# Convolution layers of a two-block network: one adding transfer per weight chunk, fewer tap sums begun on TensorE

## Chip, cores and metric

One core of a Trainium2 chip runs the whole program in one launch. The metric is the device time of one execution in microseconds (us); lower is better.

## What is computed

Two blocks on a sequence of 512 tokens with 1024 features, all in float32. The first block has four layers: a convolution layer (a), a forgetting attention (b), a short convolution (c), and a second convolution layer (a). The second block is a sparse attention with an MLP. The change touches only the two layers a:

```python
def conformer_conv_mixer(h, w_in, conv_w, conv_b, ln_g, ln_b, w_out):
    proj = h @ w_in                              # (512, 1024) @ (1024, 3 * 2048)
    val, glu_gate, z = jnp.split(proj, 3, axis=-1)
    u = val * jax.nn.sigmoid(glu_gate)
    u = causal_depthwise_conv(u, conv_w) + conv_b    # 31 taps per channel
    u = jax.nn.silu(layer_norm(u, ln_g, ln_b))
    return (u * jax.nn.silu(z)) @ w_out
```

## The kernel before

**Products in three parts.** Activations and weights are each split into a high part, rounded to the matmul's faster number format, and a low part, the rest. A product is three matmuls: high by high, high weight by low activation, low weight by high activation. The weights arrive in chunks of 1 MB (`specs`), which alternate between two raw slots in `WR`, two in `WH` and two in `WL`. A chunk of the layers a has two halves of 128 columns: in the first 16 chunks the gate's columns and the value's, in the next 8 two tiles of z.

`load_chunk` runs on the sync queue (SP) and fills a raw slot, as soon as the low parts of the chunk that lay there before are done. `split_hi` on ScalarE copies a half to `WH` (that is the rounding) and, for the halves named by `summed`, writes its negative to `WL` too. `split_lo` on GpSimd then makes the low part: for those halves by a transfer that adds the raw weights to `WL` (`dma_add`, 512 KB, semaphores `w_sum`), for the others by a subtraction (semaphore `w_lo`). `wait_low` is the wait of the readers, TensorE and the sync queue, for either. In before, both halves of the chunks 1 to 15 of a layer are done by transfers, of the z chunks the first half by a transfer and the second by a subtraction.

**The slots of a layer.** Channels lie on partitions, in 16 tiles of 128. The work runs in slots 0 to 32. In slot s below 16 TensorE makes the gate and the value of tile s (`gemm_low_last`: 16 matmuls with the high weights, then a wait, then 8 with the low), ScalarE the sigmoid, VectorE the product `U[s]`. In slots 16 to 29 TensorE makes z, one tile a slot; ScalarE writes its silu (`silu_z`). TensorE may start slot s once `U[s - 2]` is made.

**The convolution.** A tile's 31 taps are summed in one of two ways. Tiles in `CHAIN` are summed in a PSUM bank by VectorE, one `stt` a tap. The sum is begun either by ScalarE with one tap (`begins_scalar`) or, for the tiles in `PE_BEGINS`, by TensorE with two taps, as matmuls of `U` with diagonal matrices that ScalarE makes (`diagonals_scalar`). The tiles in `POOL_TAPS` are summed by GpSimd: ScalarE writes the product of each tap (`products_scalar`) into a ring of 7 buffers, and GpSimd adds it (`conv_gpsimd`). A tile there with fewer than 30 taps is shared: GpSimd adds so many, VectorE the rest. Finished tiles are turned on TensorE (`turn_u`) for the layer norm's moments on VectorE.

**What sets the order.** `conv_plan` writes down, before anything runs, which taps, adds, beginnings and turns fall in which slot: `room` taps for VectorE and `room` adds for GpSimd, alternating between at most two tiles. Every engine then runs its part of each slot in program order. On ScalarE a slot below 16 is: second half of the next chunk (high, negative), start of a tile, first half of the products, sigmoid, first half of the chunk after next, beginnings, second half of the products. In a z slot it is: a half chunk, `silu_z`, then all products. On GpSimd a slot below 16 is: transfer of the next chunk's second half, half of the adds, transfer of the first half of the chunk after next, the other adds. The functions in question are `summed` (L321), `wait_low` (L325), `split_hi` (L360), `split_lo` (L373), the constants (L888 to L892), `conv_plan` (L896) and `layer_a_gpsimd` (L1313).

Of the kernel before, what the change touches and what calls it, by code (L numbers as in the profile page):

```python
# [18 lines left out]
KE = E // P  # L19
# [3 lines left out]
PAD = TAPS - 1  # L23
# [97 lines left out]
def build_program(nc, x, a_norm, a_w_in, a_conv_w, a_conv_b, a_ln_g, a_ln_b, a_w_out, b_norm,  # L121
# [4 lines left out]
    with ctx:  # L126
# [15 lines left out]
        WL = sb("WL", 2 * 2048, F32R)  # L142
# [66 lines left out]
        specs = []  # L209
# [22 lines left out]
        FIRST_A = [0, 0]  # L232
# [61 lines left out]
        def raw_slot(i):  # L294
            return WR[:, slot_of(i) * 2048:(slot_of(i) + 1) * 2048]
# [21 lines left out]
        w_hi, w_lo = sig("w_hi"), sig("w_lo")  # L317

        w_sum = [[sig(f"w_sum{i}{n}") for n in range(2)] for i in range(2)]

        def summed(i, n):  # L321

            return i == 0 and n == 1 or any(f < i < f + KE + (KE // 2 if n == 0 else 0) or i == f + KE + KE // 2 + 1 for f in FIRST_A)

        def wait_low(eng, i, n):  # L325
            if summed(i, n):
                eng.wait_ge(w_sum[i % 2][n], i)
            else:
                eng.wait_ge(w_lo, i, n)
# [41 lines left out]
                        act.act(halves(WL, i)[n], r, ACT.Copy, scale=-1.0).then_inc(w_hi, i, n, "low")  # L371

        def split_lo(pool, i, which=(0, 1)):  # L373
            if i < len(specs):
                for n, (r, h, l) in enumerate(zip(halves(WR, i), halves(WH, i), halves(WL, i))):
                    if n not in which:
                        continue
                    if summed(i, n):
                        pool.wait_ge(w_hi, i, n, "low")
                        if two_runs(i):  # L380
                            l, r = (t.rearrange("p k c -> p (k c)") for t in (l, r))
                        pool.dma_add(l, r).then_inc(w_sum[i % 2][n], i, by=16)
                    else:
                        pool.wait_ge(w_hi, i, n)
                        pool.tt(l, r, h, ALU.subtract).then_inc(w_lo, i, n)
# [499 lines left out]

        POOL_TAPS = {2: PAD, 4: PAD, 7: PAD, 10: PAD, 12: 24}  # L888
        CHAIN = [i for i in range(KE) if POOL_TAPS.get(i, 0) < PAD]
        PE_BEGINS = CHAIN[3:]  # L890
        LAST_TAP = {i: PAD - 2 if i in PE_BEGINS else PAD - 1 for i in CHAIN}
        BY_PE = [(i, k) for i in PE_BEGINS for k in (PAD, PAD - 1)]  # L892
        POOLED = sorted(POOL_TAPS)
        Z_LATE = 3

        def conv_plan():  # L896
# [5 lines left out]
            for slot in range(2 * KE + 1):  # L902
                rest = slot == 2 * KE
# [18 lines left out]
                while begun < len(CHAIN) and begin() is not None:  # L922
                    at["begin"].append(CHAIN[begun])
                    open_.append(CHAIN[begun])
                    begun += 1
                room = PAD * KE if rest else (15) if slot < KE else (7)
                for n in range(room):
                    two = [i for i in open_ if taps[i]][:2]
                    if two:
                        i = two[n % len(two)]  # L930
# [3 lines left out]
                for i in POOLED:  # L934
                    if i < slot and i not in pooled and len([m for m in pooled if adds[m]]) < 2:
                        pooled.append(i)
                        at["start"].append(i)
                room = PAD * KE if rest else (8) if slot < KE else (3 + slot % 2)
                for n in range(room):
                    two = [i for i in pooled if adds[i] and (adds[i][0] < PAD or emptied.get(i, slot) < slot)]  # L940
                    if two:
                        i = two[n % len(two)]
# [370 lines left out]
        def layer_a_gpsimd(pool, j):  # L1313
            c0 = FIRST_A[j]
            normalise_gpsimd(pool, j)

            def pads():
                if j == 0:
                    biases_gpsimd(pool)
                    pool.wait_ge(bias_mm)  # L1320
                    pool.wait_ge(x0, KD - 1)
                else:
                    pool.wait_ge(p_out, 2, 7)
                    pool.wait_ge(x_new, 2, KD - 1)
                pool.memset(AR[:, 0:KE * UW].rearrange("p (i u) -> p i u", i=KE)[:, :, 0:PAD], 0.0).then_inc(
                    consts, "a_pads", j)

            if j:
                pads()
            for slot in range(2 * KE + 1):  # L1330
                n = PLAN[slot]["add"]
                if slot < KE:
                    split_lo(pool, c0 + slot + 1, (0, 1) if slot == 0 else (1,))
                    if j == 0 and slot == 0:
                        pads()
                    conv_gpsimd(pool, j, n[:len(n) // 2])
                    split_lo(pool, c0 + slot + 2, (0,))
                    conv_gpsimd(pool, j, n[len(n) // 2:])
                else:
                    m = (slot - KE) // 2  # L1340
                    if slot < 2 * KE - Z_LATE and slot % 2 == 0:
                        split_lo(pool, c0 + KE + m + 1, (1,))
                    elif slot < 2 * KE - Z_LATE and m + 2 < KE // 2:
                        split_lo(pool, c0 + KE + m + 2, (0,))
                    conv_gpsimd(pool, j, n)
            split_lo(pool, c0 + KE + KE // 2)
            for i in range(0, KE, 2):
                part_low(pool, 3 * j, i, U[i][:, PAD:])
                if i == 0:
                    split_lo(pool, c0 + KE + KE // 2 + 1)  # L1350
                if i >= 4:
                    split_lo(pool, c0 + KE + KE // 2 + i // 2)
            split_lo(pool, c0 + KE + KE)
            for k in range(KD):
                scale_gpsimd(pool, 3 * j + 1, SQUARES[3 * j + 1], k)
# [1633 lines left out]
```

## Time and profile before

| | us |
|---|---|
| time, median of 3 runs (2595.8 to 2599.55) | 2596.78 |
| the profiled execution | 2595.92 |
| its span, first to last instruction | 2594.2 |
| TensorE busy | 2549.5 (98%) |
| VectorE busy | 1509.1 (58%) |
| GpSimd busy | 1514.1 (58%) |
| ScalarE busy | 1231.4 (47%) |
| the 16 DMA engines, share of the span: queue of the sync engine | 31.0% |
| the same, queue of GpSimd | 10.0% |

PE is TensorE (PEld its loading of weights), DVE VectorE, ACT ScalarE, POOL GpSimd, SP the sync engine; a q behind it is that engine's queue. L64 is the line of the helper that issues every matmul, L70 that of every ScalarE operation, L73 that of every operation on two tensors, L81 that of VectorE's taps, L115 the adding transfer, L118 the weight load. `out<-in` names tiles: WR, WH and WL are raw, high and low weights, HH and HL high and low activations, AR the arena with `U`, the products and the sums, SQ and DG further product buffers, ps a PSUM bank. A group of equal instructions has a count (x8) and its whole stretch as its time. The granted clock of TensorE was 0.997 of the full 2.4 GHz on the mean. Layer 0 lies from about 40 to 320 us, layer 1 from about 1445 to 1733 us.

### The profile page before, as it was taken

To read this page: it belongs to the slowest core of one execution; us is meant where nothing else is said; L and a number is where in the kernel's file an instruction comes from. 1 tells how busy PE (TensorE), PEld (TensorE's weight loads), DVE (VectorE), ACT (ScalarE), POOL (GpSimd) and SP (SyncE) were. 2 spreads that over 40 slices of the span, in tenths; PEclk is the share of its full clock that TensorE was granted. 3 is DMA by queue.
4 is the path that set the end of the run, shared out by engine and by line. 5 is a ranking of instruction groups with operands and counts; after the bars stand their busy time and mean duration, and the time that the engine had idled before them with its cause. 6 is when DMAs were issued, how large, how long until landed. Compare 5 with 4: busy or idle time off the path is not lost.

```text
span 2594.2 us, 31715 instructions
## 1 busy us (share of the span) xinstructions
PE 2549.5 (98%) x12043; PEld 2053.2 (79%) x12043; DVE 1509.1 (58%) x2434; ACT 1231.4 (47%) x1944; POOL 1514.1 (58%) x935
## 2 busy tenths in 40 slices
PE   8999999999999999999999999999999999999998
PEld 6777787878777787888888877878876778788887
DVE  6999764165585714444450899976498743532202
ACT  5887644254564633222232688754335553422322
POOL 2999765444444366444455499966535547644653
PEclk9999999999999999999999999999999999999999
DMA  8776434434334123333333677543422242233221
GB/s 196 177 177 144 121 96 93 98 81 76 77 75 74 57 98 86 96 96 97 97 98 98 155 169 179 132 114 109 114 94 85 67 139 97 85 98 98 98 98 65
DMA packets 296439, 279.12 MB, mean 108 GB/s; under 512 B 17813, under 2 KB 258671, under 8 KB 296288
## 3 DMA queue, kind: packets, MB, share of 16 engines
q1 hardware_dynamic: 281472, 223.94, 31.0%
q0 software_dynamic: 14816, 53.16, 10.0%
q8 instruction: 96, 1.57, 0.3%
q14 instruction: 55, 0.45, 0.1%
HBM read 228.75 MB, written 5.84 MB: 90 GB/s over the span
## 4 chain that ended last, share of the span: by engine, by line
PE 82%; DVE 11%; ACT 3%; issue 2%; DMA 1%; POOL 1%; SPq 0%; DVEq 0%; POOLq 0%; ACTq 0%
PE ps L64 80%; DVE AR L81 4%; DVE AR L73 2%; DVE ps L81 2%; PE ps L67 2%; DVE HL L81 1%; ACT L70 1%; ACT AR L70 1%; ACT HT L70 1%; DMA WR<-in_a_w_in 1%; DVE X L73 1%; POOL AR L73 0%; ACT HH L70 0%; DVE ST L97 0%; SPq L118 0%
## 5 line engine op out<-in xcount | busy, mean ns | idle before, releaser
L73 POOL TENSOR_TENSOR WL<-WR,WH 128x1024 fp32r<-128x1024 f32 x324 | 818.7, 2547 | 763.1 <-ACT WH L70 763.1
L64 PE MATMUL ps<-HH,WH 128*128 128x512 f32 x3080 | 1224.9, 398 | 4.2 <-ACT HH L70 1.2
L64 PE MATMUL ps<-HL,WH 128*128 128x512 f32 x3080 | 1193.1, 390 | 1.3 <-DVE HL L81 1.3
L64 PE MATMUL ps<-HH,WL 128*128 128x512 f32 x3080 | 1094.4, 390 | 2.4 <-DMA WL<-WR 2.3
L64 PEld LDWEIGHTS ps<-HH,WH 128*128 128x128 f32 x3080 | 578.7, 188 | 146.8 <-issue 16.2
L64 PEld LDWEIGHTS ps<-HL,WH 128*128 128x128 f32 x3080 | 579.2, 188 | 126.6 <-issue 7.9
L64 PEld LDWEIGHTS ps<-HH,WL 128*128 128x128 f32 x3080 | 578.0, 188 | 124.4 <-DMA WL<-WR 2.8
L70 ACT ACTIVATE WH<-WR 128x1024 fp32r<-128x1024 f32 (+1 forms) x405 | 409.2, 1047 | 486.3 <-PE ps L64 443.0
L81 DVE SCALAR_TENSOR_TENSOR ps<-AR,CW,ps 128x512 f32<-128x512 f32 x654 | 454.5, 751 | 18.4 <-ACT ps L70 11.4
L73 POOL TENSOR_TENSOR AR<-AR 128x512 f32<-128x512 f32 x200 | 306.2, 1831 | 17.3 <-ACT AR L70 10.1
L70 ACT ACTIVATE AR<-ps 128x512 f32<-128x512 f32 (+3 forms) x265 | 132.0, 522 | 272.1 <-PE ps L64 175.9
L73 DVE TENSOR_TENSOR AR<-AR 128x512 f32<-128x512 f32 (+1 forms) x161 | 212.1, 1346 | 39.4 <-ACT AR L70 37.8
L64 PE MATMUL ps<-AR 128*64 128x128 f32 (+17 forms) x1450 | 217.9, 346 | 14.9 <-DVE AR L81 8.3
L73 DVE TENSOR_TENSOR HL<-AR,HH 128x512 fp32r<-128x512 f32 x57 | 76.1, 1346 | 197.4 <-ACT HH L70 192.5
L73 DVE TENSOR_TENSOR AR<-ps,HT 128x512 f32<-128x512 f32 (+1 forms) x70 | 47.8, 687 | 244.6 <-PE ps L64 224.5
L64 PEld LDWEIGHTS ps<-AR 128*128 128x128 f32 (+6 forms) x1450 | 132.7, 169 | 69.6 <-issue 41.9
L115 POOL DMA_DIRECT2D WL<-WR x81 | 103.6, 1278 | 68.7 <-ACT WL L70 68.7
L70 ACT ACTIVATE AR<-AR 128x512 f32<-128x512 f32 (+3 forms) x72 | 41.0, 588 | 198.3 <-DVE AR L73 192.0
L73 POOL TENSOR_TENSOR AR<-AR,SQ 128x512 f32<-128x512 f32 x80 | 131.1, 1877 | 1.3
L73 DVE TENSOR_TENSOR AR<-AR,HT 128x512 f32<-128x512 f32 x48 | 70.2, 1462 | 101.1 <-ACT AR L70 100.6
L73 DVE TENSOR_TENSOR X<-X,ps 128x512 f32<-128x512 f32 x48 | 32.4, 681 | 148.5 <-PE ps L64 148.3
L70 ACT ACTIVATE AR<-AR,CW 128x512 f32<-128x512 f32 x168 | 110.9, 713 | 1.8 <-POOL AR L73 1.8
(184 smaller groups left out, 2178.4 us busy)
## 6 DMA issues: line engine op xcount, KB each, us to landing
WR<-in_a_w_in SPq DMA_DIRECT2D x96, 512.0 KB, 5.2
WL<-WR POOLq DMA_DIRECT2D x81, 512.0 KB, 5.7
WR<-in_c_w_in SPq DMA_DIRECT2D x64, 512.0 KB, 5.3
WR<-in_a_w_out SPq DMA_DIRECT2D x16, 1024.0 KB, 4.9
WR<-in_b_w_in SPq DMA_DIRECT2D x16, 1024.0 KB, 8.6
WR<-in_b_w_in SPq DMA_DIRECT2D x32, 512.0 KB, 11.4
WR<-in_w_mlp_in SPq DMA_DIRECT2D x16, 1024.0 KB, 5.4
WR<-in_w_mlp_out SPq DMA_DIRECT2D x16, 1024.0 KB, 5.0
```

The source lines that it names most:

```text
L64: return Op(None if self.e is None else self.e.matmul(o, l, r, start=first, stop=last, skip_group_check=True))
L67: return Op(None if self.e is None else self.e.transpose(o, i, identity))
L70: return Op(None if self.e is None else self.e.activation(o, i, f, **kw))
L73: return Op(None if self.e is None else self.e.tensor_tensor(o, a, b, op))
L81: return Op(None if self.e is None else self.e.scalar_tensor_tensor(o, a, s, b, op0, op1))
L115: return Op(None if self.e is None else self.e.dma_start(o, i, accum_op=ALU.add))
```

## The change

For the chunks 1 to 23 of each layer a, both halves now have their low part by one joint transfer of 1 MB (`joint`). It is issued once ScalarE has written the negatives of both halves, and everybody who waits for either half waits for it. In slots below 16 GpSimd issues it for the next chunk after three adds of its slot; in even z slots after two. Tile 12 is now summed by GpSimd wholly, tile 14 shared with 8 taps. TensorE begins every second of the later tiles in `CHAIN`, ScalarE the others. The plan's room is 14 or 15 taps (VectorE) and 8 or 9 adds (GpSimd) a slot below 16, and 7 and 4 in z slots.

```diff
         def summed(i, n):
 
-            return i == 0 and n == 1 or any(f < i < f + KE + (KE // 2 if n == 0 else 0) or i == f + KE + KE // 2 + 1 for f in FIRST_A)
+            return i == 0 and n == 1 or joint(i) or any(i == f + KE + KE // 2 + 1 for f in FIRST_A)
+
+        def joint(i):
+
+            return any(f < i < f + KE + KE // 2 for f in FIRST_A)
 
         def wait_low(eng, i, n):
-            if summed(i, n):
+            if joint(i):
+                eng.wait_ge(w_sum[i % 2][1], i)
+            elif summed(i, n):
                 eng.wait_ge(w_sum[i % 2][n], i)
             else:
                 eng.wait_ge(w_lo, i, n)
@@
         def split_lo(pool, i, which=(0, 1)):
-            if i < len(specs):
+            if i < len(specs) and joint(i):
+                if 1 in which:
+                    for n in range(2):
+                        pool.wait_ge(w_hi, i, n, "low")
+                    pool.dma_add(WL[:, (i % 2) * 2048:(i % 2 + 1) * 2048], raw_slot(i)).then_inc(w_sum[i % 2][1], i, by=16)
+            elif i < len(specs):
                 for n, (r, h, l) in enumerate(zip(halves(WR, i), halves(WH, i), halves(WL, i))):
@@
-        POOL_TAPS = {2: PAD, 4: PAD, 7: PAD, 10: PAD, 12: 24}
+        POOL_TAPS = {2: PAD, 4: PAD, 7: PAD, 10: PAD, 12: PAD, 14: 8}
         CHAIN = [i for i in range(KE) if POOL_TAPS.get(i, 0) < PAD]
-        PE_BEGINS = CHAIN[3:]
+        PE_BEGINS = CHAIN[3::2]
@@
-                room = PAD * KE if rest else (15) if slot < KE else (7)
+                room = PAD * KE if rest else (14 + slot % 2) if slot < KE else (7)
@@
-                room = PAD * KE if rest else (8) if slot < KE else (3 + slot % 2)
+                room = PAD * KE if rest else (8 + slot % 2) if slot < KE else (4)
@@
             for slot in range(2 * KE + 1):
                 n = PLAN[slot]["add"]
+                m = (slot - KE) // 2
                 if slot < KE:
-                    split_lo(pool, c0 + slot + 1, (0, 1) if slot == 0 else (1,))
+                    conv_gpsimd(pool, j, n[:3])
+                    split_lo(pool, c0 + slot + 1)
                     if j == 0 and slot == 0:
                         pads()
-                    conv_gpsimd(pool, j, n[:len(n) // 2])
-                    split_lo(pool, c0 + slot + 2, (0,))
-                    conv_gpsimd(pool, j, n[len(n) // 2:])
+                    conv_gpsimd(pool, j, n[3:])
+                elif slot < 2 * KE - Z_LATE and slot % 2 == 0 and m + 1 < KE // 2:
+                    conv_gpsimd(pool, j, n[:2])
+                    split_lo(pool, c0 + KE + m + 1)
+                    conv_gpsimd(pool, j, n[2:])
                 else:
-                    m = (slot - KE) // 2
-                    if slot < 2 * KE - Z_LATE and slot % 2 == 0:
-                        split_lo(pool, c0 + KE + m + 1, (1,))
-                    elif slot < 2 * KE - Z_LATE and m + 2 < KE // 2:
-                        split_lo(pool, c0 + KE + m + 2, (0,))
                     conv_gpsimd(pool, j, n)
```

## Rows read from the trace of the kernel before

**Rows 1.** Chain of waits, layer 0: start us, us, what, count.

```profile
165.14 12.64 PE ps L64 x52
...
228.34 10.92 PE ps L64 x48
239.26 0.44 PE ps L67 x4
...
292.31 5.47 PE ps L64 x24
```

**Rows 2.** Busy us of each engine by stretch, layer 0 and layer 1.

```profile
core 0: us, PE busy (x) PEld busy (x) DVE busy (x) ACT busy (x) POOL busy (x), PEclk, DMA share, GB/s
...
66.00:306.00 240.00, 234.87 (x1030) 187.01 (x1028) 226.30 (x384) 187.77 (x277) 230.90 (x184) 1.00 0.68 162
...
1490.00:1720.00 230.00, 228.92 (x1009) 183.30 (x1007) 215.79 (x368) 181.31 (x267) 222.90 (x178) 1.00 0.67 159
```

**Rows 3.** Groups of instructions, 40 to 306 us: busy us, mean ns, idle before.

```profile
L81 DVE SCALAR_TENSOR_TENSOR ps<-AR,CW,ps 128x512 f32<-128x512 f32 x327 | 227.2, 751 | 12.2 <-ACT ps L70 8.6
...
L73 POOL TENSOR_TENSOR WL<-WR,WH 128x1024 fp32r<-128x1024 f32 x10 | 26.8, 2689 | 0.0
```

**Rows 4.** Timeline of GpSimd, layer 0: start us, us, instruction, count.

```profile
150.45 1.45 POOL L115 DMA_DIRECT2D WL<-WR  x1
151.06 5.88 POOL L73 TENSOR_TENSOR AR<-AR 128x512 f32<-128x512 f32 x4
156.02 1.75 POOL L115 DMA_DIRECT2D WL<-WR  x1
```

**Rows 5.** Timeline of GpSimd, layer 1, slots 3 and 4.

```profile
1475.14 0.85 POOL L115 DMA_DIRECT2D WL<-WR  x1 [1.95 <-ACT WL L70]
1479.29 5.41 POOL L73 TENSOR_TENSOR AR<-AR 128x512 f32<-128x512 f32 x4 [3.31 <-ACT AR L70]
1486.89 0.87 POOL L115 DMA_DIRECT2D WL<-WR  x1 [2.20 <-ACT WL L70]
```

**Rows 6.** Timeline of ScalarE, layer 1: the start of tile 2's sum.

```profile
1477.71 0.82 ACT L70 ACTIVATE AR<-AR,VB,CW 128x512 f32<-128x512 f32 x1 [2.87 <-DVE AR L73]
```

**Rows 7.** Timeline of TensorE, layer 1: low matmuls of slot 4's gate.

```profile
1487.14 1.98 PE L64 MATMUL ps<-HH,WL 128*128 128x512 f32 x8
```

**Rows 8.** Timeline of TensorE and ScalarE in z slot 20, layer 0.

```profile
243.21 1.98 PE L64 MATMUL ps<-HH,WL 128*128 128x512 f32 x8
...
245.23 0.60 ACT L70 ACTIVATE AR<-ps 128x512 f32<-128x512 f32 x1 [1.37 <-PE ps L64]
...
245.72 0.71 ACT L70 ACTIVATE DG<-AR,CW 128x512 f32<-128x512 f32 x1
246.34 1.32 ACT L70 ACTIVATE AR<-AR,CW 128x512 f32<-128x512 f32 x2
```

**Rows 9.** DMA queues and landings, 239.6 to 252.8, then 264.1 to 275 us.

```profile
q0 software_dynamic: 144, 0.52, 21.0%
...
WL<-WR POOLq DMA_DIRECT2D x1, 512.0 KB, 4.4
...
WL<-WR POOLq DMA_DIRECT2D x1, 512.0 KB, 5.5
```

**Rows 10.** Landings of the adding transfers issued between 180 and 215 us.

```profile
DMA to landing us min/median/max: 5.0/6.9/8.8
```

**Rows 11.** A weight load around 191.2 us, first and last start, landings, ScalarE's copies.

```profile
L118 SPq DMA_DIRECT2D WR<-in_a_w_in x2: 367/468/570, 191.0 to 191.4; - x2
...
DMA to landing us min/median/max: 4.1/4.8/5.4
...
187.22 1.05 ACT L70 ACTIVATE WH<-WR 128x1024 fp32r<-128x1024 f32 x1
188.16 1.05 ACT L70 ACTIVATE WL<-WR 128x1024 fp32r<-128x1024 f32 x1
...
197.55 1.05 ACT L70 ACTIVATE WH<-WR 128x1024 fp32r<-128x1024 f32 x1
```

**Rows 12.** Waits, 40 to 306 us: in total, times, longest.

```profile
ACT WH L70 <- DMA WR<-in_a_w_in: 7.6, 4, 3.4
...
PE ps L64 <- DMA WL<-WR: 2.3, 1, 2.3
```

## The prediction

> **What bounds the kernel now.** I read the chain of waits first, for the two convolution layers alone, since nothing else is touched. The reader is to see that from about 104 us on the chain of layer 0 runs through TensorE with hardly a break: each slot of the first phase (16 of them) is 48 large matmuls in 10.92 us, each slot of the second phase (z) is 24 in 5.47 us, a turn of a finished tile costs 0.44, and where a tile's tap sum is begun on TensorE, four more records stand in the piece: 12.64 for 52 against 10.92 for 48 [rows 1]. So one beginning (two matmuls) costs 1.72 us of path. Then the busy table by stretch: TensorE is 98% and 99.5% busy in the two layers, but VectorE 226 of 240 us, GpSimd 231 and ScalarE 188 are close behind [rows 2]. A saving on TensorE therefore counts only until the next thing is late, and I looked for what delivers the low weights.
>
> **What TensorE, VectorE, GpSimd and ScalarE gain and lose.** The plan of the slots, worked out for both settings, gives per layer:
> TensorE begins 4 tiles (5, 8, 11, 14) where it began 9: five fewer, 5 x 1.72 = 8.6 us off the path. None of it comes before slot 7 (tile 5 stays); three (5.2 us) come in slots 7 to 15, two (3.4 us) in the z slots.
> VectorE does 318 taps where it did 327, at 227.2 / 327 = 0.69 us: 6.3 us less. In layer 0 it leads the chain up to slot 6, but there it saves only three taps (2.1 us), and the waits below cover that; later it lies beside TensorE, so I book nothing.
> GpSimd: an add is 1.24 us from start to start (four between 151.06 and 156.02), a transfer's issue 0.61 (150.45 to 151.06) [rows 4], a subtraction of a half at most the 2.69 of its mean [rows 3]. 14 adds more cost 17.4 us; 8 subtractions (of the z chunks' second halves) go, at most -21.5; 40 transfer issues become 25, -9.2 if a joint one takes no longer to issue, 0 if it takes twice that on the 23 joint ones and more. The engine ends between 13 us lighter and about even: it is no new bound as a total.
> ScalarE: 14 products at 0.62 and 8 negated copies at 0.95 more, four initial taps and fewer diagonals: about +18 us on 188 of 240 [rows 2, 8, 11]. In a z slot that is 4 products, the output's 0.49 and two copies on average, 4.9 of 5.47 us. It fits.
>
> **What a joint transfer costs.** In before, half 0 of the next-but-one chunk was sent a slot early, each half on its own. Now one transfer of 1 MB carries both halves. It can only be issued once ScalarE has copied the second half, which waits for TensorE's previous slot, and it stands behind three adds (two in z slots) on GpSimd; and TensorE needs it for the last third of the first gemm, not of the second. Its landing time L is in no row. In z slots a lone transfer of 512 KB lands after 4.4 to 5.5 us; the queue's packets fill 21.0% of 16 engines over 13.2 us for 0.52 MB, so 2.77 us of it is moving data [rows 9]. The second half megabyte adds that much again: L = 7.2 to 8.3. In a busy stretch the half's median is 6.9 [rows 10], so 9.7 there; from below the bound is 4.4 to 5, if the wider rows came free. I take 7.5, nearest the quiet rows, since fewer transfers will overlap. The Trainium skill (DMA: Bandwidth & Descriptors, section on the anatomy of one DMA on the SWDGE path) fits a transfer by 2.0 us plus its bytes over 436 GB/s and advises 1 MiB at a time; by it a joint one would take 4.4 us (estimate from that page), and the change would gain. The trace disagrees for this kind: by the same fit a half would take 3.2 us, the rows show 4.4 and more.
>
> **Where the joint transfer ends late.** Layer 1 shows it undisturbed.
> (a) Early, at slots 4 and 5. GpSimd's first adds on tile 2 start at 1479.29, 1.35 us each (5.41 for four, all on one tile). Before, chunk 4's second half left at 1475.14, ahead of them [rows 5]. Now the joint one leaves after three adds, at 1483.4, and those adds can't be earlier, since ScalarE waits until 1477.71 for VectorE's u of tile 2 [rows 6]. It lands at 1490.9; TensorE wants it at 1487.14 [rows 7]: a wait of 3.8 us. Slot 5 would start at 1490.9 + 1.82 + 5.46 = 1498.2 and want its low weights at 1501.8. GpSimd gets the products of slot 3's second half only at 1486.89, behind the load that ScalarE waits for [rows 5]; five adds of slot 3 and three of slot 4, 1.4 each, put the next joint transfer at about 1498.5, landing at 1506.0: another 4.2. From slot 6 the adds alternate between two tiles and the lag holds. Together L + 0.5 = 8 us. Layer 0 has the same order at 60 to 90 us, and I book the same.
> (b) Slots 7 to 15: the raw weights. The sync queue may load a raw slot again only when the sums from it have landed. The two parts of a load are issued at 191.0 and 191.4, the last landing 5.4 us later, at 196.8, and ScalarE starts its copy at 197.55 [rows 11]: 0.7 us of slack now, and four times it already waits, 7.6 us in all [rows 12]. With the joint transfer the loop over two slots is L, load 5.8, four copies at 0.95, some 4.5 products, begins and evacuations 0.65 (estimate), three products 1.9, an add 1.24: L + 16.2 = 23.7 us. TensorE's own nine slots would take 9 x 10.92 + 3 x 1.72 + 6 x 0.44 = 106.1, or 23.6 for two. So the loop and TensorE are level; with overlap of transfers I book 2 us per layer, between 0 (L = 7.2) and 5 (L = 8.3).
> (c) Z slots. There ScalarE makes the slot's products only after it has passed on the finished z: low matmuls from 243.21 to 245.03, output at 245.23, products at 245.72 and 246.34, each 0.71 long [rows 8]. GpSimd's two adds then run until 248.95 and the joint transfer leaves 3.9 us after the end of z. TensorE meanwhile has the odd z (5.47), a turn (0.44) and 16 of the next 24 matmuls (3.64): 9.55 us. Wait per pair of slots: 3.9 + L - 9.55 = L - 5.65, at 7.5 some 1.9 us. Before, the halves were sent or subtracted ahead of all adds. Slots 16 to 26 have six such: 11.2 us.
> The late chunk of z, the layer norm and the output projection keep their order: nothing.
>
> **Sum.** Per layer -8.6 + 8 + 2 + 11.2 = +12.6 us, for two +25. The profiled execution took 2595.9 us (span 2594.2) and lies 0.9 below the median: 2621 by it, 2622 against the median. Written with L, a layer costs 7L - 42 plus (b): with 7.2 and 0 it is +8.4 (total 2613), with 8.3 and 5 it is +21 (2638). The likeliest case's own range is 2608 to 2645.
>
> **Rivals.**
> 1. Faster, in full: the joint transfers are never late, the 17 us of TensorE stay: 2579. For it speaks that the chain is TensorE from 104 us on; against it that the three adds ahead of the transfer can't be earlier than row 1479.29. 6%.
> 2. Faster, in part: a joint transfer lands as soon as a half, 5 us at most. Then z never waits (from L = 5.65 down), the early waits are 1.3 + 4.2, per layer -8.6 + 5.5 = -3.1: 2590. This is what the skill's page named above would lead to; against it stands the 2.77 us of data in [rows 9]. 8%.
> 3. No change: L near 6, where 7L - 42 is zero: 2597. It needs a transfer of which the second half costs 1.5 us. 8%.
> 4. Much slower: landing as in the busy stretch, 9.7 us; 7 x 9.7 - 42 = 26 and 8 or more from (b), per layer 34: 2665. For it speaks that ScalarE already waits for loads. 8%.
> 5. The forecast, 70%.
> That the change wouldn't do what it says has no room: both plans follow from the listed constants.
>
> **How the numbers follow.** The likeliest case gives 2622. What a measurement can tell from no change is about 0.2%, 5 us. Faster: rivals 1 and 2, 14%. Same: rival 3, 8%. Slower: the forecast and rival 4, 78%. The range takes in the forecast's bounds and reaches down to rivals 2 and 3: 2590 to 2645; out of it stay rival 1, rival 4 and a little of the forecast, some 20%.
>
> **What would show it.** In the waits of TensorE, "DMA WL<-WR" must rise from one wait of 2.3 us [rows 12] to some 15 with 15 to 25 us per layer; in the z slots the chain must alternate: z, ScalarE, GpSimd adds, transfer. Chain pieces with 52 matmuls must be 4 a layer. A joint transfer's landing must read 7 to 8.5 us. If landings read under 6, or GpSimd's issue of them comes before the three adds' products in time, the forecast is wrong; if ScalarE's wait for weight loads grows past 20 us per layer, (b) is too small.

## The result, and the profile after

The changed kernel takes 2653.7 us (median of 4 runs, 2650.8 to 2656.9), the kernel before beside it 2597.0: a ratio of 1.0217, 95% interval 1.0204 to 1.023. The profiled execution has a span of 2649.1 us against 2594.2. It is slower, as forecast, but by 57 us where 25 were forecast, and the time lies outside the range.

The page of after: busy time, three groups, and the landing of the joint transfers.

```profile
PE 2551.8 (96%) x12003; PEld 2052.7 (77%) x12003; DVE 1499.5 (57%) x2416; ACT 1264.3 (48%) x1976; POOL 1485.0 (56%) x917
...
L73 POOL TENSOR_TENSOR WL<-WR,WH 128x1024 fp32r<-128x1024 f32 x308 | 775.0, 2537 | 775.6 <-ACT WH L70 775.6
...
L64 PE MATMUL ps<-HH,WL 128*128 128x512 f32 x3080 | 1109.0, 395 | 55.5 <-DMA WL<-WR 55.4
...
L81 DVE SCALAR_TENSOR_TENSOR ps<-AR,CW,ps 128x512 f32<-128x512 f32 x636 | 441.3, 752 | 21.4 <-ACT ps L70 14.7
...
WL<-WR POOLq DMA_DIRECT2D x46, 1024.0 KB, 7.0
```

The low matmuls (HH with WL) now wait 55.4 us in the whole execution for the adding transfers, where they waited 2.3 us before. GpSimd's subtractions are 308 for 324, the 16 second halves of z chunks that went. VectorE does 636 taps, 318 a layer, as the plan said (327 in [rows 3] was one layer of before). And a joint transfer lands after 7.0 us: the forecast's L, 7.2 to 8.3 and taken as 7.5, was right in size and slightly too long.

To see where the time lies I cut each layer at three matmuls: the low ones of slot 7's gate, of the first z slot and of the fourteenth. These are the stretches of after, layer 0 and then layer 1 (the columns are those of [rows 2]).

```profile
40.00:118.40 78.40, 71.02 (x291) 56.74 (x290) 69.55 (x100) 57.19 (x80) 48.50 (x41) 0.94 0.68 158
118.40:237.10 118.70, 110.00 (x470) 87.51 (x469) 98.69 (x169) 94.72 (x137) 103.45 (x86) 0.97 0.70 165
237.10:326.10 89.00, 78.51 (x338) 62.70 (x337) 70.58 (x119) 62.95 (x91) 66.01 (x55) 0.96 0.64 149
```

```profile
1484.20:1559.90 75.70, 68.76 (x296) 55.05 (x297) 67.62 (x99) 52.82 (x74) 47.19 (x40) 1.00 0.73 167
1559.90:1677.80 117.90, 109.12 (x470) 86.85 (x470) 97.80 (x165) 94.67 (x138) 103.51 (x86) 0.97 0.69 161
1677.80:1764.10 86.30, 76.95 (x337) 61.72 (x336) 70.62 (x119) 64.22 (x92) 66.36 (x56) 0.98 0.69 164
```

And the same stretches of layer 0 in the kernel before:

```profile
40.00:108.00 68.00, 63.84 (x279) 50.85 (x277) 65.32 (x95) 51.50 (x74) 44.69 (x40) 1.00 0.81 178
108.00:218.70 110.70, 110.70 (x477) 87.60 (x476) 107.03 (x175) 92.54 (x137) 110.47 (x95) 1.00 0.76 176
218.70:295.80 77.10, 77.10 (x345) 62.45 (x345) 72.25 (x126) 53.73 (x79) 75.63 (x57) 1.00 0.54 130
```

Two things are to be seen. TensorE was busy without a gap from slot 7 on and has gaps now. And the granted clock, 1.00 in every stretch before, reads 0.94 to 0.98 in five of six now. The waits of TensorE for WL in the same six stretches of after, in the same order (us in total, times, longest), are:

```profile
PE ps L64 <- DMA WL<-WR: 7.4, 3, 3.9
...
PE ps L64 <- DMA WL<-WR: 8.7, 3, 4.3
...
PE ps L64 <- DMA WL<-WR: 10.5, 6, 3.1
...
PE ps L64 <- DMA WL<-WR: 8.1, 5, 2.3
...
PE ps L64 <- DMA WL<-WR: 8.8, 3, 5.0
...
PE ps L64 <- DMA WL<-WR: 9.4, 6, 2.5
```

The 8.1 of the fourth line counts a wait of 1.1 us that ends where its stretch begins; inside the stretch are 6.9 (75.70 less 68.76). The waits ahead of slot 7 are those for the chunks of slots 2, 3 and 5 in layer 0 (0.7, 2.8 and 3.9 us, after one of 2.7 us at slot 1, ahead of the stretch), and of slots 3, 4, 5 and 6 in layer 1 (1.0, 2.3, 1.9 and 1.7 us).

### The profile page after: what moved, and what is told of

Its sections match the earlier page's. It is cut to its first block, busy times and chain, and to the rows that moved or that the text cites. A ratio compares the mean times of both kernels' runs of the same rounds, so it can differ in the third digit from the quotient of the medians.

```text
span 2649.1 us, 31650 instructions
## 1 busy us (share of the span) xinstructions
PE 2551.8 (96%) x12003; PEld 2052.7 (77%) x12003; DVE 1499.5 (57%) x2416; ACT 1264.3 (48%) x1976; POOL 1485.0 (56%) x917
## 3 DMA queue, kind: packets, MB, share of 16 engines
q1 hardware_dynamic: 281472, 223.94, 30.3%
## 4 chain that ended last, share of the span: by engine, by line
PE 65%; DMA 11%; DVE 10%; ACT 7%; issue 4%; POOL 3%; SPq 0%; DVEq 0%; POOLq 0%; ACTq 0%
PE ps L64 64%; DMA WL<-WR 8%; DVE AR L81 4%; DMA WR<-in_a_w_in 3%; POOL AR L73 3%; ACT AR L70 2%; DVE AR L73 2%; PE ps L67 2%; DVE HL L81 1%; ACT L70 1%; ACT WL L70 1%; ACT WH L70 1%; ACT HT L70 1%; ACT SQ L70 1%; DVE X L73 1%
## 5 line engine op out<-in xcount | busy, mean ns | idle before, releaser
L73 POOL TENSOR_TENSOR WL<-WR,WH 128x1024 fp32r<-128x1024 f32 x308 | 775.0, 2537 | 775.6 <-ACT WH L70 775.6
L64 PE MATMUL ps<-HH,WL 128*128 128x512 f32 x3080 | 1109.0, 395 | 55.5 <-DMA WL<-WR 55.4
L81 DVE SCALAR_TENSOR_TENSOR ps<-AR,CW,ps 128x512 f32<-128x512 f32 x636 | 441.3, 752 | 21.4 <-ACT ps L70 14.7
L73 POOL TENSOR_TENSOR AR<-AR 128x512 f32<-128x512 f32 x216 | 291.0, 1391 | 70.5 <-ACT AR L70 63.1
L64 PE MATMUL ps<-AR 128*64 128x128 f32 (+15 forms) x1410 | 197.9, 338 | 16.3 <-DVE AR L81 8.2
L64 PEld LDWEIGHTS ps<-AR 128*128 128x128 f32 (+5 forms) x1410 | 124.4, 168 | 65.6 <-issue 36.7
L73 DVE TENSOR_TENSOR AR<-ps,AR 128x512 f32<-128x512 f32 (+4 forms) x104 | 67.8, 659 | 108.8 <-PE ps L64 106.8
L73 POOL TENSOR_TENSOR AR<-AR,SQ 128x512 f32<-128x512 f32 x88 | 118.9, 1394 | 13.7 <-ACT SQ L70 12.7
L70 ACT ACTIVATE AR<-AR,CW 128x512 f32<-128x512 f32 x184 | 120.7, 711 | 0.0
```

The source lines that it names most:

```text
L64: return Op(None if self.e is None else self.e.matmul(o, l, r, start=first, stop=last, skip_group_check=True))
L70: return Op(None if self.e is None else self.e.activation(o, i, f, **kw))
L73: return Op(None if self.e is None else self.e.tensor_tensor(o, a, b, op))
L81: return Op(None if self.e is None else self.e.scalar_tensor_tensor(o, a, s, b, op0, op1))
```

## The experiments

All stretches in us, each read from the one profiled execution of its kernel, to about 0.1. "7 to z" runs from slot 7's gate to the first z slot, "z" covers 13 z slots. The first column is the time at which slot 7's gate is reached in layer 0, and in layer 1 the time from slot 1's gate to it. Ratios are to the kernel before, run beside each.

| kernel | time | ratio (95%) | layer 0: to 7, 7 to z, z | layer 1: 1 to 7, 7 to z, z |
|---|---|---|---|---|
| before | 2597.0 | | 108.0, 110.7, 77.1 | 68.0, 110.7, 77.1 |
| after | 2653.7 | 1.0217 (1.0204-1.0230) | 118.4, 118.7, 89.0 | 75.7, 117.9, 86.3 |
| 1 z first | 2628.6 | 1.0119 (1.0104-1.0134) | 119.9, 119.1, 73.5 | 75.6, 118.1, 73.8 |
| 2 slots first | 2626.5 | 1.0112 (1.0097-1.0127) | 117.3, 105.9, 87.1 | 75.3, 105.9, 86.3 |
| 3 both first | 2599.8 | 1.0012 (1.0003-1.0021) | 116.4, 105.9, 73.8 | 75.8, 106.2, 73.5 |
| 4 plan only | 2621.0 | 1.0091 (1.0074-1.0108) | 109.1, 108.3, 84.7 | 67.5, 110.6, 83.4 |
| 5 joint only | 2644.6 | 1.0190 (1.0174-1.0205) | 116.7, 114.1, 85.3 | 79.1, 112.5, 86.1 |
| 6 halves, same place | 2631.8 | 1.0135 (1.0121-1.0149) | 115.4, 120.6, 76.6 | 76.3, 118.2, 78.3 |
| 7 early halves | 2591.9 | 0.9980 (0.9971-0.9989) | 108.6, 111.7, 73.5 | 67.5, 113.0, 73.8 |
| 8 four adds | 2673.7 | 1.0292 (1.0278-1.0306) | 121.4, 123.3, 89.5 | 80.2, 123.3, 86.5 |
| 9 two ahead | 2626.4 | 1.0114 (1.0100-1.0128) | 108.2, 117.7, 81.3 | 67.5, 124.7, 82.6 |
| 10 joint, two ahead | 2636.6 | 1.0158 (1.0144-1.0172) | 115.5, 118.1, 81.2 | 74.3, 117.8, 82.0 |
| 11 z joint only | 2602.8 | 1.0026 (1.0015-1.0038) | 109.1, 114.4, 75.6 | 67.5, 114.6, 76.8 |
| 12 switch at 6 | 2593.4 | 0.9986 (0.9977-0.9996) | 114.2, 105.8, 73.6 | 73.2, 105.9, 73.8 |

Stretches that never wait take 105.9 and 73.5 to 73.8 (kernel 3). Against before's 110.7 and 77.1 that is 8.1 us a layer, the beginnings that TensorE no longer does: forecast 5.2 + 3.4 = 8.6.

**1 and 2: which adds does the transfer wait behind?** Kernel 1 sends the joint transfer of a z slot ahead of its adds, kernel 2 that of a first-phase slot.

```
# kernel 1, z slots                       # kernel 2, slots below KE
-    conv_gpsimd(pool, j, n[:2])          -    conv_gpsimd(pool, j, n[:3])
     split_lo(pool, c0 + KE + m + 1)           split_lo(pool, c0 + slot + 1)
-    conv_gpsimd(pool, j, n[2:])          -    conv_gpsimd(pool, j, n[3:])
+    conv_gpsimd(pool, j, n)              +    conv_gpsimd(pool, j, n)
```

> The changed kernel, with the joint transfer of a z slot issued before that slot's adds; the slots below 16 stay as they are. Theory A (the transfer's place behind two adds, whose products ScalarE makes only after it has passed on the finished z, costs TensorE its waits in z): z slots 16 to 29 took 94.5 us in the changed kernel against a PE-bound 79; without the two adds ahead the transfer leaves about 7 us earlier, no wait is left, so some 14 us per layer go: 2654 - 28 = 2626 (2618 to 2634). Rival B (GpSimd's extra adds bound the z slots): the order within a slot changes nothing, 2650 or more. Rival C (the landing time itself, 7 us, is what is too long wherever it stands): at most 5 us per layer, 2644 or more.

> The changed kernel, with the joint transfer of a slot below 16 issued before that slot's adds; the z slots stay as they are. Theory A (below slot 16 the loop of two slots is landing 7.0, load 5.7, first copies 1.9, a first product 0.7 and then seven or eight adds of GpSimd at 1.24 before the next transfer of the same raw slot, 25 to 26 us against TensorE's 23.6): three adds fewer in the loop bring it under TensorE's time, and the early waits at slots 4 and 5 go too. Slot 16 starts some 18 us earlier than in the changed kernel in layer 0 and some 12 to 18 in layer 1: 2654 - 32 = 2622 (2614 to 2632). Rival B (ScalarE's pace in that loop, or the DMA traffic, sets it): ScalarE's 14 more products stay, so at most the 8 us of the early waits per layer go, 2638 or more. Rival C (GpSimd is simply full): nothing, 2650 or more.

Measured: 25 and 27 us less than after, both within what was expected. Each edit repairs exactly its own stretch: the z stretch falls by 15.5 and 12.5 us, in kernel 2 the stretch from slot 7 by 12.8 and 12.0. Kernel 2 leaves the early loss (117.3 against 108.0) nearly as it was, though its theory A had the early waits go too.

**3: both.**

> The changed kernel with both transfers ahead of the adds, in all slots. Theory A: what is left is TensorE's saving of 17 us and a few us of late transfers in the first slots: 2654 - 28 - 32 = 2594 by the parts, down to 2582 if no wait at all is left; 2588 taken. It would be the fastest so far. Rival B (GpSimd's load): over 2620.

Measured: 2599.8, 12 us above the expectation. The two gains add (54 of the 57 us), and from slot 7 on the layers run as the forecast's best case. What stays is 8.4 and 7.8 us ahead of slot 7, which the forecast had put down to the three adds. There are none ahead of the transfer now, so that reason was wrong. The chain of kernel 3 at the start of layer 0 shows another:

```profile
52.84 0.69 DVE AR L73
...
53.56 0.69 ACT ps L70
54.26 0.98 ACT WH L70
55.23 0.96 ACT WL L70
...
56.73 7.73 DMA WL<-WR
...
64.89 9.27 DMA WR<-in_a_w_in
```

The joint transfer leaves right behind ScalarE's copy of the second half, and that copy stood in ScalarE's queue behind a sum's start that waited for VectorE. In before the copy stood there too. Its first half had been sent long ago, and its second left at nearly the same time as the joint transfer of kernel 3. GpSimd of before:

```profile
56.10 0.85 POOL L115 DMA_DIRECT2D WL<-WR  x1 [9.96 <-ACT WL L70]
```

That one landed after 4.6 us, and the raw slot's next load was issued at 60.7; the joint one takes 7.7, and the load is issued at 64.5. So the place of the copy is not what differs: the joint transfer lands later, and holds back the next load of raw weights as well. In layer 1 two joint transfers of 6.9 to 7.0 us stand on the chain ahead of loads in the same way (from 1450.91 and 1473.93).

**4 and 5: the two parts of the change alone.** Kernel 4 has the new tap plan with the transfers as before, kernel 5 the transfers with the plan as before.

```
-        POOL_TAPS = {2: PAD, 4: PAD, 7: PAD, 10: PAD, 12: 24}
+        POOL_TAPS = {2: PAD, 4: PAD, 7: PAD, 10: PAD, 12: PAD, 14: 8}
-        PE_BEGINS = CHAIN[3:]
+        PE_BEGINS = CHAIN[3::2]
-                room = PAD * KE if rest else (15) if slot < KE else (7)
+                room = PAD * KE if rest else (14 + slot % 2) if slot < KE else (7)
-                room = PAD * KE if rest else (8) if slot < KE else (3 + slot % 2)
+                room = PAD * KE if rest else (8 + slot % 2) if slot < KE else (4)
```

This diff against before is the whole of kernel 4; kernel 5 is after with these four lines taken back.

> The kernel before with only the new plan (fewer beginnings on TensorE, tile 12 and 8 taps of tile 14 on GpSimd, 14 or 15 taps and 8 or 9 adds a slot); the halves are sent and subtracted one by one as before. Theory A (all of the loss lies in the joint transfers): the 17 us of TensorE show, less what GpSimd is late at the end, since a pair of z slots is 8 adds, a transfer's issue and a subtraction, 12.9 us against TensorE's 11.4: 2580 to 2592, 2587 taken. Rival B (the 28 more adds and products are what costs): slower than before, 2610 or more.

> The kernel before with only the joint transfers, at the places where the change has them; plan, beginnings and GpSimd's adds are those of before. Theory A (place of the transfer, priced by GpSimd's adds): the first slots cost as in the changed kernel (10 and 8 us in the two layers); the loop of two slots has seven adds, 25.3 us against the 24.6 that TensorE needs with its nine beginnings, so 4 us per layer; z costs 9 to 12 us per layer, since two beginnings there hide part of two waits. 2597 + 2 x 22 = 2641 (2632 to 2650). Rival B (the joint transfers alone cost all of the change's loss, the plan only saves): 2654 + 17 = 2671. Rival C (the loss needs GpSimd's extra adds): under 2620.

Kernel 5 came as expected (+47 us for the joint transfers at the change's places). Kernel 4 was a miss: 2621, not 2587, and in the range of its rival B, by which the added adds and products are what costs. Up to slot 7 it is on time, but with the subtractions of the z chunks still on GpSimd that engine has 8 adds, a subtraction and an issue for each pair of z slots, 8 x 1.24 + 2.4 + 0.6 = 12.9 us against TensorE's 11.4. The subtraction's length is from this row of GpSimd's timeline, three of them in a row:

```profile
309.00 7.25 POOL L73 TENSOR_TENSOR WL<-WR,WH 128x1024 fp32r<-128x1024 f32 x3
```

The waits of kernel 4 over z and the tail of layer 0 say who is late:

```profile
ACT AR L70 <- POOL AR L73: 12.4, 7, 4.2
...
PE ps L67 <- POOL AR L73: 4.1, 1, 4.1
```

It also ends z late: from the fourteenth to the next low matmuls 14.5 us where the others take 8.1. So the joint transfers, which take eight subtractions off GpSimd, are what makes room for the 14 adds; neither half of the change pays alone.

**6: size or place?** After, with each joint transfer issued as two of 512 KB at the same place; each half is waited for by itself (that edit isn't shown).

```
-                    pool.dma_add(WL[:, (i % 2) * 2048:(i % 2 + 1) * 2048], raw_slot(i)).then_inc(w_sum[i % 2][1], i, by=16)
+                    for n, (r, l) in enumerate(zip(halves(WR, i), halves(WL, i))):
+                        l, r = (t.rearrange("p k c -> p (k c)") for t in (l, r))
+                        pool.dma_add(l, r).then_inc(w_sum[i % 2][n], i, by=16)
```

> The changed kernel with the joint transfer split again into two of 512 KB, both issued where the joint one was, and each waited for by itself. Theory A: a half lands after 4.5 to 5 us, below the 5.65 from which a z slot waits, so the z waits go, 13 us per layer; in the slots below 16 the raw slot is free only when the second half has landed, some 7.5 us after the issue as before, so the loop stays at 26 us and gains nothing, perhaps loses 2 us per layer for the second issue: 2654 - 26 + 4 = 2632 (2624 to 2640). Rival B (only the place counts, a half is waited for as long): 2650 or more. Rival C (the size is all): both stretches gain, 2610 or less.

Measured 2631.8, as expected. In z the first half lands in time and most of the wait goes (76.6 and 78.3). From slot 7 on nothing is won (120.6 and 118.2). That fits the expectation, by which the loop over the raw slot waits for the second half there as it did for the joint transfer.

**8: one more add ahead of the transfer in the first phase.**

```
-                    conv_gpsimd(pool, j, n[:3])
+                    conv_gpsimd(pool, j, n[:4])
```

> The changed kernel with four adds instead of three ahead of the joint transfer in the slots below 16; z as in the changed kernel. Theory A (GpSimd's adds, 1.24 us each, are links of the two-slot loop): 1.24 us more per two slots, 4.5 times per layer, 5.6 us per layer: 2654 + 11 = 2665, all of it between slots 7 and 16. Rival B (ScalarE's pace, 0.62 us a product): 2654 + 5.5 = 2659. Rival C (landing and load alone set the loop): 2654.

Measured 2673.7, 20 us more than after, more than any theory gave. The stretch from slot 7, 4.5 turns of the two-slot loop, grows by 4.6 and 5.4 us: 1.0 to 1.2 us a turn, one add. Another 3.0 and 4.5 us lie in the early slots.

**7: halves early, joint transfers from chunk 8.** Kernel 3, with chunks 1 to 7 as halves at before's places.

```
-    return i == 0 and n == 1 or joint(i) or any(i == f + KE + KE // 2 + 1 for f in FIRST_A)
+    return i == 0 and n == 1 or joint(i) or any(f < i < f + 8 or i == f + KE + KE // 2 + 1 for f in FIRST_A)
-    return any(f < i < f + KE + KE // 2 for f in FIRST_A)
+    return any(f + 8 <= i < f + KE + KE // 2 for f in FIRST_A)
@@ slots below KE
+    split_lo(pool, c0 + slot + 1, (0, 1) if slot == 0 else (1,))
+    conv_gpsimd(pool, j, n[:len(n) // 2])
+    split_lo(pool, c0 + slot + 2, (0,))
+    conv_gpsimd(pool, j, n[len(n) // 2:])
```

> The kernel with both transfers ahead of the adds (e3), but the chunks 1 to 7 of each layer sent in halves, at the places of the kernel before; joint ones only from chunk 8 on. Theory A (in e3 the only loss left, 8 us per layer up to slot 7, comes from the joint transfers of the first chunks, which wait for ScalarE's second half and hold back the next load): slot 7 starts when it does in the kernel before, and TensorE's saving of 8.4 us per layer is left: 2600 - 16 = 2584, at best 2580; faster than both kernels. Rival B (the first slots are late by the plan, by fewer taps and more adds): no gain against e3, 2597 or more.

Measured 2591.9, faster than both kernels by a little (0.2%), and 8 us short of the expectation. Slot 7 is on time now (108.6 and 67.5), but the loss comes back behind it, 5.8 and 7.1 us over 105.9. TensorE in layer 0:

```profile
119.00 0.39 PE L64 MATMUL ps<-HH,WH 128*128 128x512 f32 x1
...
122.73 3.78 PE L64 MATMUL ps<-HH,WL 128*128 128x512 f32 x8 [2.66 <-DMA WL<-WR]
126.30 0.63 PE L64 MATMUL ps<-HH,WH 128*128 128x512 f32 x1
...
131.19 1.98 PE L64 MATMUL ps<-HH,WL 128*128 128x512 f32 x8
```

The chain that led there:

```profile
111.97 0.88 POOL AR L73
...
114.44 8.24 DMA WL<-WR
```

And the stretch behind it (the columns of [rows 2], the granted clock third from the end):

```profile
122.70:128.80 6.10, 6.07 (x14) 4.78 (x15) 6.10 (x13) 4.57 (x8) 6.02 (x6) 0.50 0.62 172
```

The first joint transfer leaves at 114.44, behind slot 6's adds, and lands 2.7 us late. Then TensorE runs at half its clock for 6.1 us (0.50 of 2.4 GHz): the low matmuls take 3.78 us for 1.98, a large one 0.63 for 0.39. From 122.73 to 131.19 are 8.46 us where the same 24 matmuls take 5.44. A wait of 2.7 us has cost 5.8.

**9 and 10: the joint transfer sent half a slot earlier.** Kernel 9 is kernel 7 with it amid the adds of the slot two before its chunk; kernel 10 does so from chunk 2 on, without halves.

```
+                    if slot < 7:
                         split_lo(pool, c0 + slot + 1, (0, 1) if slot == 0 else (1,))
                     conv_gpsimd(pool, j, n[:len(n) // 2])
-                    split_lo(pool, c0 + slot + 2, (0,))
+                    if slot < KE - 1:
+                        split_lo(pool, c0 + slot + 2, (0, 1) if slot >= 6 else (0,))
```

> The version with halves for chunks 1 to 7 and joint transfers from chunk 8, of which each joint transfer is now sent one half slot earlier: in the middle of the adds of the slot two before its chunk, not at the start of the adds of the slot one before. Theory A (a joint transfer of the first phase is late because it stands behind adds that GpSimd still owes, and a wait of 3 us costs 6, since TensorE's clock falls to half after it): chunk 8's second copy is done at 109.2 us, so the transfer leaves at about 109.5 instead of 114.4, lands at 116.7 and TensorE wants it at 119.9; the wait and the half-clock stretch behind it go, 5.8 us in layer 0 and 7 in layer 1 of the stretch from slot 7 to the first z slot: 2580, between 2577 and 2585. Rival B (GpSimd now waits for ScalarE's second copy and its adds come later, so that z or the accumulation is late instead): 2592 to 2600.

> The same place in the middle of the adds, two chunks ahead, but joint transfers from chunk 2 on, no halves. Theory A (in the first slots it is the joint form itself that is late: it waits for the second half's copy, which waits for TensorE's previous slot, and lands 2.5 us later than a half): slots 1 to 6 still lose 4 to 8 us a layer against the version with early halves, and so 2590, between 2586 and 2596. Rival B (only the place in GpSimd's queue mattered, early too): the same as the version with early halves sent at this place, 2580.

Both missed: 2626 and 2637, where 2580 and 2590 were expected. In kernel 9 the first joint transfer does leave earlier (110.84), but the next one, and then every one, waits for ScalarE. GpSimd and ScalarE of kernel 9:

```profile
117.72 4.54 POOL L73 TENSOR_TENSOR AR<-AR 128x512 f32<-128x512 f32 x3
125.05 0.88 POOL L115 DMA_DIRECT2D WL<-WR  x1 [2.79 <-ACT WL L70]
```

```profile
123.46 1.04 ACT L70 ACTIVATE WL<-WR 128x1024 fp32r<-128x1024 f32 x1
129.83 0.81 ACT L70 ACTIVATE AR<-AR,VB,CW 128x512 f32<-128x512 f32 x1 [5.33 <-POOL AR L73]
```

GpSimd stands 2.8 us for the copy with its adds queued behind, and ScalarE then stands 5.3 us for those adds: rival B, and at 30 us dearer than I had priced it. The place in the queue has an optimum, not a direction: behind adds the transfer is late, ahead of ScalarE's copy the adds are. Kernel 10 loses 7.5 and 6.3 us before slot 7 as well, so there it is the joint form that is late, wherever it stands.

**11 and 12: the change of form made elsewhere.** Kernel 7 with the joint form from chunk 16 (z only), and from chunk 6.

```
-    return any(f + 8 <= i < f + KE + KE // 2 for f in FIRST_A)
+    return any(f + KE <= i < f + KE + KE // 2 for f in FIRST_A)      # kernel 11
+    return any(f + 6 <= i < f + KE + KE // 2 for f in FIRST_A)       # kernel 12
```

> The new plan with halves, sent and placed as in the kernel before, for all chunks of the first phase, and joint transfers in the z slots alone, sent ahead of the adds. Theory A (halves carry the first phase, the joint form is needed only in z, where it takes the subtractions off GpSimd): the stretch from slot 7 to the first z slot takes its 105.9 plus the 2.4 and 4.7 us which the plan alone showed there, z takes 73.5 to 74.5 and the tail is on time; of the 17 us 7 are lost in the first phase and some 3 at the first z slots: 2590, between 2586 and 2593. Rival B (the first joint transfer costs its 6 to 7 us a layer wherever the change of form is made): 2596 or more.

> The version with early halves, joint transfers starting with chunk 6 instead of chunk 8; all else the same. Theory A (the change of form from halves to joint is paid once a layer, some 6 us wherever it is made, a wait and the half-clock stretch behind it, and is cheaper only where something other than TensorE leads): in layer 0 VectorE leads up to slot 7, TensorE has 3 us of slack at slot 6 and 1 to 2 at slot 7, so some 3 us of the 6 are hidden; in layer 1 there is no such slack and it costs the same 7: 2589, between 2585 and 2592. Rival B (the cost grows with the number of joint transfers in the first phase, so that two more cost more): 2594 or above.

Kernel 11 takes 2602.8, as its rival B had it (its profiled execution, from which the stretches are, took 2606.4), and kernel 12 2593.4. The low matmuls at the change of form, of kernel 11 and then of kernel 12:

```profile
223.48 3.24 PE L64 MATMUL ps<-HH,WL 128*128 128x512 f32 x8 [4.38 <-DMA WL<-WR]
```

```profile
99.10 3.78 PE L64 MATMUL ps<-HH,WL 128*128 128x512 f32 x8 [8.31 <-DMA WL<-WR]
```

Counted against stretches without a wait, the change of form costs 8.4 and 7.8 us a layer at chunk 1 (kernel 3), 6.2 and 5.7 at chunk 6 (by slot 7: 114.2 against 108.0, 73.2 against 67.5), 5.8 and 7.1 at chunk 8. In kernel 11 the two steps around the first z slot take 12.2 and 7.2 us where kernel 3 takes 7.6 and 5.4, so 6.4; in layer 1 they take 11.6 and 7.1, so some 5.7. Behind it no wait for WL is longer than 0.6 us in any of the four. It is paid once a layer, wherever it is made (in kernel 3 spread over the waits of slots 1 to 5), and two more joint transfers cost nothing more. By its time alone kernel 12 lies between its theory (up to 2592) and its rival B (2594 or above); it is the stretches, 105.8 and 105.9 us behind the change, that speak against the rival. The slack that I had hoped for in layer 0 at slot 6 hid nothing, since the transfer there was later by as much (8.3 us). Kernel 11 has another 3.9 and 4.7 us between slot 7 and its switch, in slots of halves under the new plan.

## Why the forecast had the direction and not the size

Its steps a layer, with what the stretches measured (layer 0, layer 1):

| step | forecast | measured | of it waits | of it clock |
|---|---|---|---|---|
| beginnings gone | -8.6 | -8.1, -8.1 | | |
| (a) early slots | +8 | +10.4, +7.7 | 7.4, 6.9 | 4.7, 0 |
| (b) slots 7 to 15 | +2 | +12.8, +11.7 | 8.7, 8.8 | 3.6, 3.5 |
| (c) z slots | +11.2 | +15.2, +12.8 | 10.5, 9.4 | 3.6, 1.7 |
| sum | +12.6 | +30.3, +24.1 | | |

The measured column is the stretch of after less that of kernel 3 (for (a), less that of before); the waits are the rows above (in (a) of layer 1 without the one that ends at its start), and the clock is the length of the stretch times what its granted clock lacks of 1.00, as 0.06 x 78.4 = 4.7. Waits and clock together give 38.5 and 30.3 us where the measured steps (a) to (c) have 38.4 and 32.2. In (a) of layer 0 the split is rough: it adds up to 12.1 for 10.4, since before itself stood still for 4.2 us there (68.00 less 63.84) and after comes into the stretch late. The two layers' 54.4 us are nearly the spans' whole difference, 54.9.

**Right:** the direction and its reason. The beginnings were sized right, L was right (7.5 for 7.0), and in z there are six waits a layer, at 1.6 to 1.75 us each where L - 5.65 gave 1.9. The chain of z alternates as written, and kernel 1, which takes the adds away, has no such wait. Chain of after, layer 0:

```profile
242.91 6.96 DMA WL<-WR
...
249.91 2.13 PE ps L64 x8
...
256.52 6.92 DMA WL<-WR
...
263.48 3.41 PE ps L64 x8
```

**The step that failed is (b),** 2 us a layer where 12 were lost. The loop over two slots was priced at L + 16.2 us: four copies and seven or eight products on ScalarE, and one add of GpSimd. One turn of it, from the chain of after in layer 1:

```profile
1606.01 7.34 DMA WL<-WR
...
1613.78 5.35 DMA WR<-in_a_w_in
...
1619.15 1.06 ACT WH L70
1620.21 0.95 ACT WL L70
1621.16 1.23 ACT AR L70 x2
1622.38 0.62 ACT SQ L70
...
1623.18 0.49 POOL AR L73
...
1630.92 1.23 POOL AR L73
1632.16 6.93 DMA WL<-WR
```

GpSimd in the same turn, up to that transfer:

```profile
1621.91 2.56 POOL L73 TENSOR_TENSOR AR<-AR 128x512 f32<-128x512 f32 x2 [2.00 <-ACT AR L70]
1624.44 2.53 POOL L73 TENSOR_TENSOR AR<-AR,SQ 128x512 f32<-128x512 f32 x2
1627.05 1.30 POOL L73 TENSOR_TENSOR AR<-AR,DG 128x512 f32<-128x512 f32 x1
1628.43 3.79 POOL L73 TENSOR_TENSOR AR<-AR 128x512 f32<-128x512 f32 x3
```

The transfer took 7.4 us to the load's issue (booked 7.5), order and load 5.8 (booked 5.8), ScalarE 3.9 for two copies and three products (booked 9.15, for four copies, products and evacuations), and GpSimd 9.15 until the next transfer (booked 1.24). The loop leaves ScalarE after two copies and runs through GpSimd. Eight adds stand there between the load and the transfer: five of the slot, and the three of `n[:3]` in the next one. ScalarE makes a product in half the time that GpSimd needs to add one, so the adds trail the products; step (a) of the same forecast counted three adds, step (b) one. That is 26.15 us for this turn, and 130.8 / 5 = 26.2 on average over five turns of layer 1 (transfers issued at 1526.88 and 1657.68), against TensorE's 23.6. All five run this way. One turn of layer 0 (174.79 to 199.67, 24.9 us) goes over all four copies as the forecast had it, and also ends behind three adds, 3.8 us of them.

A loop that is 2.6 us too long loses that on every one of 4.5 turns: 11.7 us, what was measured in layer 1. The forecast had called the loop "level" with TensorE, and at that point an error of 2.5 us in it counts 4.5 times. Kernel 2 takes the three adds out and leaves the five in, 22.5 us by this count (estimate, 26.2 less 3 x 1.24), and has no wait; kernel 8 (a fourth) pays 1.0 to 1.2 us more a turn.

**The forecast had no term for the clock.** It priced each wait at its length. The rows show that TensorE comes out of nine of its 27 waits in the two layers at half its clock: in z the eight low matmuls behind one take 3.41 us instead of some 2, and in kernel 7 the stretch of 6.1 us stands at 0.50. The same run has waits with the clock kept up: behind one of 2.77 us, at 1664.60, the next low matmuls follow after 5.6 us, behind one of 3.58 us, at 222.26, after 7.2. The Trainium skill (TensorE: Matmul & The Clock Gate, section on oscillation) tells of the same cycle, a wait for data that sends the array into the next tile cold, there at every tile. The trace agrees for nine of the 27 waits. By the table the clock accounts for 17 of the 70 us lost in both layers. Not all of that makes the kernel longer by itself: the chain of the five turns in (b) of layer 1 has no piece of TensorE, and there the loop's length alone gives the 11.7 us. Some 7 of the 17 us lie in (b). No run holds the clock up with the waits as they are, so what the clock costs beyond the waits isn't shown by an experiment.

**(a) was right in size by a wrong reason, which is luck.** It argued from three adds, put waits of 3.8 and 4.2 us at slots 4 and 5, and came to L + 0.5. The waits are spread over slots 1 to 6 (above). Kernels 2 and 3 took the adds away and 7.3 to 9.3 us stayed, though a fourth add costs 3.0 and 4.5 us there (kernel 8); kernels 7, 9, 4 and 11, with halves in these slots, lost under 1.2. The cause is the joint form: it carries both halves only once the second is copied, and its longer landing delays the next load. Kernels 7, 11 and 12 show further that this isn't a matter of the early slots but a lag that TensorE takes on once, at the first joint transfers.

**Of the signs named in the forecast** two spoke: ScalarE's wait for weight loads is 31.8 us over layer 0 and 35.1 over layer 1 ([rows 12] had 7.6 in all), over the 20 that were to show (b) too small; and TensorE's waits for WL are 12 in layer 0 and 14 in layer 1, at 26.6 and 26.3 us, where 15 to 25 us were named. Rival 4 (2665) was nearest in number, but not in kind: it needed L of 9.7, and L is 7.0.

## What to carry to other kernels

When a step's loop comes out level with the bound, write out its chain instruction by instruction and count everything queued ahead of the critical issue, what is left of the previous slot too; each microsecond too much returns on every turn. A wait of a TensorE that was running without gaps can cost more than its length: behind nine of 27 here its clock was halved. Before joining two transfers, ask what the first half bought by leaving early; and move a transfer in an in-order queue neither behind work that can wait nor ahead of data that isn't there yet: here each cost over 1%.

## What the runs showed of the hardware

- An adding transfer from SBUF to SBUF of 1 MB lands after 7.0 us in the median (46 of them). In the z slots one of 512 KB took 4.6 (7 of before) and one of 1 MB 7.0 (7 of after): 2.4 us for the second half, near the 2.77 read from the queue in [rows 9]. In slots 7 to 15, where the halves overlap with more, the medians are 6.5 (19) and 7.1 (10). The issue on GpSimd takes 0.6 us for either size (a joint one at 174.79, the next add at 175.40).
- A wait of TensorE of 1.92 us (ahead of the matmuls at 263.48 in after) was followed by half clock, eight matmuls in 3.39 us; one of 1.93 us two slots later (ahead of 278.67) was not, eight in 2.11. Which waits bring the fall can't be said from these runs.
- Two kernels of the study beat the kernel before, with intervals that leave no change out: kernel 7 by 0.2% and kernel 12 by 0.1%. Of the 16 us that the new plan frees on TensorE 12 to 13 are spent on the two lags of the joint form. A switch without a lag wasn't found.
